# Gate and up columns of two feed-forward blocks: a new order of high-part and low-part matmuls

## What is computed

```python
def swiglu(h, w_gate, w_up, w_down):
    return (jax.nn.silu(h @ w_gate) * (h @ w_up)) @ w_down
...
    h = h + swiglu(rmsnorm(h, norm_ffn[i]), w_gate[i], w_up[i], w_down[i])
...
    h = rmsnorm_2(x, norm_ffn[i])
    up = dwconv3(h @ ffn_w_up[i], ffn_conv_w[i], ffn_conv_b[i])
    gate, val = jnp.split(up, 2, axis=-1)
    x = x + (jax.nn.silu(gate) * val) @ ffn_w_down[i]
```

## Time and profile before

| what | value |
|---|---|
| runs shown | 2710.66, 2700.53, 2703.84 us |
| median | 2703.84 us |
| profiled execution, its own time | 2710.54 us |
| its span | 2708.7 us |
| mean granted TensorE clock | 0.992 of full |
| TensorE busy | 2639.3 us (97%) |
| VectorE busy | 1924.6 us (71%) |
| ScalarE busy | 1495.4 us (55%) |

### The profile page before, as it was taken

One profiled execution on the slowest core, in us unless ns is written; L12 is line 12 of the kernel. 1 busy time (PEld: TensorE's weight loads), 2 busy tenths in 40 slices (PEclk: granted clock), 3 DMA queues, 4 the chain that ended last, 5 costly groups with the idle time before them and its releaser, 6 DMA issues.

```text
span 2708.7 us, 38546 instructions
## 1 busy us (share of the span) xinstructions
PE 2639.3 (97%) x14978; PEld 2276.8 (84%) x14978; DVE 1924.6 (71%) x2916; ACT 1495.4 (55%) x2307; POOL 393.6 (15%) x391
## 2 busy tenths in 40 slices
PE   7999999999998999999999999999999999999997
PEld 7888888888887888888888888888888888888886
DVE  8677786777787665656565679687877767676775
ACT  6555566768555444444444456535555555555554
POOL 3011100413411001010101033011101010101012
PEclk9999999999998999999999999999999999999999
DMA  7556666656554555666666656536566666666653
GB/s 247 163 184 183 184 196 193 188 184 188 172 177 133 168 162 172 188 192 187 188 191 189 188 162 211 167 117 187 179 194 190 190 188 189 190 189 189 189 179 121
DMA packets 135838, 490.76 MB, mean 181 GB/s; under 512 B 15207, under 2 KB 15528, under 8 KB 135656
## 3 DMA queue, kind: packets, MB, share of 16 engines
q1 hardware_dynamic: 135656, 488.31, 59.1%
HBM read 486.12 MB, written 2.13 MB: 180 GB/s over the span
## 4 chain that ended last, share of the span: by engine, by line
PE 87%; DVE 8%; ACT 2%; issue 2%; DMA 0%; DVEq 0%; ACTq 0%; SPq 0%
PE ps L708 56%; PE ps L710 28%; DVE wl L1195 3%; ACT wh L913 1%; DVE hT L1195 1%; DVE X L1201 1%; PE ps L849 0%; PE ps L882 0%; DVE R L1195 0%; DVE Gf L1195 0%; DVE T L1195 0%; DVE A L1201 0%; DVE A L1195 0%; DVE T L1201 0%; PE ps L795 0%
## 5 line engine op out<-in xcount | busy, mean ns | idle before, releaser
L1195 DVE TENSOR_TENSOR wl<-raw,wh 128x1024 fp32r<-128x1024 f32 x902 | 1140.8, 1269 | 710.3 <-ACT wh L913 709.6
L708 PE MATMUL ps<-X,wh 128*128 128x512 f32 x4848 | 1538.4, 399 | 5.5 <-DVE hT L1195 3.5
L913 ACT ACTIVATE wh<-raw 128x1024 fp32r<-128x1024 f32 x902 | 952.3, 1059 | 951.2 <-PE ps L710 931.0
L710 PEld LDWEIGHTS ps<-X,wl 128*128 128x128 f32 x4848 | 912.7, 188 | 215.1
L710 PE MATMUL ps<-X,wl 128*128 128x256 f32 x4848 | 955.7, 278 | 0.0
L708 PE MATMUL ps<-XG,wh 128*128 128x512 f32 x2304 | 734.1, 400 | 31.1 <-DVE hT L1195 17.0
L708 PEld LDWEIGHTS ps<-X,wh 128*128 128x128 f32 x4848 | 742.6, 189 | 20.1 <-issue 8.7
L710 PEld LDWEIGHTS ps<-XG,wl 128*128 128x128 f32 x2304 | 435.8, 189 | 103.4
L710 PE MATMUL ps<-XG,wl 128*128 128x256 f32 x2304 | 455.5, 279 | 0.0
L1650 POOL TENSOR_TENSOR hT<-hT,T 128x256 f32<-128x256 f32 x224 | 190.2, 870 | 1459.0 <-DVE hT L1195 1459.0
L708 PEld LDWEIGHTS ps<-XG,wh 128*128 128x128 f32 x2304 | 353.9, 190 | 39.1 <-DVE hT L1195 20.4
(11 more groups left out here) (168 smaller groups left out, 1105.2 us busy)
## 6 DMA issues: line engine op xcount, KB each, us to landing
raw<-in_w_gate SPq DMA_DIRECT2D x176, 512.0 KB, 3.7
raw<-in_w_down SPq DMA_DIRECT2D x176, 512.0 KB, 3.7
raw<-in_w_sc SPq DMA_DIRECT2D x96, 512.0 KB, 4.1
raw<-in_w_up SPq DMA_DIRECT2D x88, 512.0 KB, 3.6
raw<-in_w_val SPq DMA_DIRECT2D x88, 512.0 KB, 3.7
raw<-in_w_zx SPq DMA_DIRECT2D x80, 512.0 KB, 3.9
raw<-in_w_in SPq DMA_DIRECT2D x68, 512.0 KB, 3.7
raw<-in_w_osc SPq DMA_DIRECT2D x32, 512.0 KB, 3.7
```

The source lines that it names most:

```text
L708: e.matmul(bank(c, i)[:, :], wh[:, b0 + 128 * i:b0 + 128 * i + 128], x, start=st and kk == 0, stop=False)
L710: t = e.matmul(bank(c, i)[:, 0:256], wl[:, b0 + 128 * i:b0 + 128 * i + 128], x[:, 0:256], start=False, stop=sp and kk == c.kn - 1)
L913: return e.activation(out, in_, ACT.Copy, scale=scale)
L1195: return e.tensor_tensor(out, a, b, op)
```

## The change

Gate and up columns no longer issue their 16 matmuls in the loop that the other columns use. The unit first waits for all four activation tiles, and then takes its matmuls from a list of triples (kk, bank, low) that `orders` gives. The sums are the same sets of products; only their order in each bank differs. The first matmul into a bank is still H with kk = 0. The unit's last matmul still increments `mm`, and the stop flag is set at the last matmul of each bank.

```diff
+def orders(which, first):
+    start, rest = which % 5, which // 5
+
+    def alternate(ks):
+        if rest == 0:
+            return [(k, i, m) for k in ks for i in range(2) for m in range(2)]
+        return [(k, i ^ m, m) for i in range(2) for k in ks for m in range(2)]
+
+    if not first:
+        return alternate(range(4))
+    if start == 0:
+        return [(k, i, m) for m in range(2) for k in (0, 1) for i in range(2)] + alternate((2, 3))
...
+    if start == 2:
+        return [(0, 0, 0), (0, 1, 0), (1, 0, 0), (0, 0, 1), (0, 1, 1), (1, 0, 1), (1, 1, 0), (1, 1, 1)] + alternate((2, 3))
+    if start == 3:
+        return [(k, i, m) for m in range(2) for k in (0, 1, 2) for i in range(2)] + alternate((3,))
...
+ORDER_OF = [5, 0, 6, 1, 7, 2, 8, 3, 9, 4, 0, 9, 1, 8, 2, 7, 3, 6, 4, 5, 8, 1, 4, 7, 0, 3, 6, 9, 2, 5, 5, 3, 1, 9, 7, 6, 0, 2, 4, 8, 3, 2, 0, 5]
...
                 w.wait_ge(s, n)
+                if c.kind in ("gate", "up"):
+                    continue
...
+            if c.kind in ("gate", "up"):
+                order = orders(ORDER_OF[c.i], st)
+                ends = {i: n for n, (kk, i, low) in enumerate(order)}
+                for n, (kk, i, low) in enumerate(order):
+                    X, kx = xtile(c, g * c.kn + kk)[:2]
+                    b0 = (u % NW) * UN + kk * 256 + 128 * i
+                    if low:
+                        t = e.matmul(bank(c, i)[:, 0:256], wl[:, b0:b0 + 128], X[:, kx * 512:kx * 512 + 256], start=False,
+                                     stop=sp and n == ends[i])
+                    else:
+                        t = e.matmul(bank(c, i)[:, :], wh[:, b0:b0 + 128], X[:, kx * 512:kx * 512 + 512], start=st and kk == 0,
+                                     stop=sp and n == ends[i])
```

More of the change, by code:

```diff
@@ L383, in schedule @@
     return at
+def orders(which, first):
[8 more added lines that the diff above has]
+        return [(k, i, m) for m in range(2) for k in (0, 1) for i in range(2)] + alternate((2, 3))
+    if start == 1:
+        return [(k, i, m) for m in range(2) for k in (0, 1) for i in range(2)] + [(2, 0, 0), (2, 1, 0), (2, 0, 1), (3, 0, 0), (
+            2, 1, 1), (3, 1, 0), (3, 0, 1), (3, 1, 1)]
+    if start == 2:
+        return [(0, 0, 0), (0, 1, 0), (1, 0, 0), (0, 0, 1), (0, 1, 1), (1, 0, 1), (1, 1, 0), (1, 1, 1)] + alternate((2, 3))
+    if start == 3:
+        return [(k, i, m) for m in range(2) for k in (0, 1, 2) for i in range(2)] + alternate((3,))
+    return [(k, i, m) for m in range(2) for k in (0, 1) for i in range(2)] + [(2, i, m) for m in range(2) for i in range(2)] + alternate((3,))
+ORDER_OF = [5, 0, 6, 1, 7, 2, 8, 3, 9, 4, 0, 9, 1, 8, 2, 7, 3, 6, 4, 5, 8, 1, 4, 7, 0, 3, 6, 9, 2, 5, 5, 3, 1, 9, 7, 6, 0, 2, 4, 8, 3, 2, 0, 5]
 PLAN = schedule()
```

## The result

The changed kernel takes 2712.26 us (median of 19 runs, 2705.62 to 2716.89), beside 2707.18 us for the kernel before on the same chips (19 runs, 2700.53 to 2710.86). The ratio is 1.0020, with a 95% interval of 1.0012 to 1.0028. So it is slower by about 5 us, less than the 0.5% that counted as a difference, and about half of the 10.9 us that the sum gave.

A forecast was written before the change was run, and what follows sets the result against it. The prediction took TensorE to bound the gate and up stretches. Alternation added 10.9 us (10.6 in later units, 0.4 in first units), waits and bank nothing: 2703.84 + 10.9 = 2714.7 us, range 2697 to 2730 us.

The forecast's parts named there:

- The bound: Gate and up stretches: TensorE bounds them, busy 997.05 of 997.17 us; every nanosecond of pitch goes straight into the time.
- The time: Whole kernel: 2714.7 us, ratio 1.004; 2711 to 2718 given 50%, "same" (within 0.5%) given 0.64.
- The cost of alternation: Gate and up units: an alternating H and L pair costs 353.3 ns against 348.3, 40 ns a whole unit.
- The prediction's own sign of being wrong: Changed gate and up columns: the forecast is wrong if a pair over two banks has any pitch but 353 ns.
- The price by steps: Gate and up units: one more HL and LH replacing HH and LL costs 10.0 ns; 1094 more HL steps, +10.9 us.
- Bounds: Limits of the alternation term: -80 us from streaming alone, -5 us at the `v` stretch's price, +33 us from above.
- The bank: Gate and up pairs: one bank or two was given no price, but kept as a rival.
- Rival 1: Gate and up: only a pair on one bank is dear, kinds 5 to 9 pay nothing; +5.7, 2709.5 us; 14%.
- Rival 2: Gate and up columns: order has no effect, the 5 ns are peculiar to `dt`; 2703.8 us; chance 10%.
- Rival 3: Gate and up: L between two H hides its load better if the bank changes; 2699 or 2691 us; chance 10%.
- Rival 4: Gate and up: changing tile, weights and bank each step makes pairs 0.36 us; up to +33 us, 2737; chance 16%.
- Waits that move ahead: First gate column of each layer: activation tiles waited for up to 2.1 us earlier; price nothing.

## Why the prediction came out as it did

*The bound* was read rightly: TensorE's pitch in the gate and up stretches goes into the time one for one, with nothing to absorb it and nothing behind it. Stretches grew by 5.2 us, the runs by 5.1.

*The time* fell into the range of 2697 to 2730 us and into "same", but the difference to the kernel before is +5.1 us and not +10.9; the range was wide enough for either. That 2712.26 us lies in the narrower forecast of 2711 to 2718 is luck: the sum started from 2703.84 us, and the median of the kernel before over 19 runs is 2707.18.

*The cost of alternation* is the step that failed, as a term: "a pair costs 5.0 ns more", from the `dt` column's 353.3 against 348.3 ns, taken for all alternating pairs "because the work is the same". It measured +5.0 ns in the long columns (47 in the second to tenth stretches) and -1.7 ns in the short ones (31). The `dt` row was a fair sample of one rhythm of two, and no row of before showed the other. Fifteen steady pairs looked like fifteen observations; they were one, since a stream in a fixed cycle repeats itself. The rows as printed could not warn of it: pairs of 0.35, 0.36 and 0.35 us are also what a fixed 353.3 ns gives when start times are rounded to 0.01 us. The whole ns of the same trace could, since the pitches of H in `dt` go 232, 241, 235 and begin again. The prediction's own sign of being wrong, a pair over two banks at anything but 353 ns, did come: kind 9 runs at 346.7.

*The price by steps* (one more HL and LH costs 10.0 ns) went with it. It gave the first units +0.4 us; they cost +0.8 in the second to tenth stretches alone. Kind 4's first unit, with as many HL steps as HHLL has, is 7 ns shorter, and that of kind 3, with fewer, is 7 ns longer.

*Bounds.* The `v` stretch's lower bound of 346.6 ns a pair is what the short rhythm has (346.7), but its parts are not: the bound has 226.6 for H and 120 for L, the short rhythm 231.5 and 115, so the sum agrees by chance. Some two in five columns met the lower bound; the sum had put them at 353.3 like the others. All units of the kernel at that pitch would be 892 x -13.3 ns = -12 us, and no repeating order here came to under it.

*The bank* was rightly given no price: the run with one bank a pair changed no unit behind the first stretch but two of gate 22. Rival 1 came nearest in time (2709.5 on a median of 2703.8), and by the wrong mechanism. *Rival 2*, that the order has no effect, doesn't hold: the same 16 matmuls took 2773, 2787, 2793 or, on average, 2827 ns by their order and entry. The 325 ns a pair worked out from the formula for an isolated matmul in the Trainium skill ("TensorE: Matmul & The Clock Gate", section "Back-to-back issue gap") is below every repeating row here, whose shortest pair is 346.7 ns. *Rival 3* was right that something faster exists, for kinds 4 and 9, but by phase and not by bank. *Rival 4* didn't come: 0.36 us pairs exist only as one of three in the long rhythm.

*Waits that move ahead* cost nothing that can be seen: the only wait in the gate and up matmuls is 1.3 us ahead of the first gate column, where the kernel before waited 2.8 us.

## What to carry to other kernels

A steady stretch in a trace is one sample of the pattern it runs in, however long it is; before its price is used elsewhere, ask whether the pattern there is entered in the same way, and look for a cycle in the single pitches. Where an engine is bound by back-to-back instructions of two lengths, their order and the way into a repeating row can be worth 1.5% of the stretch (88.82 against 90.20 us), with no instruction more or less; a short lead-in that ends in the good phase is the whole edit. Here versions with such a lead-in beat both kernels (0.9980 to 0.9990 of the kernel before), but it must be tried, since a lead-in works only if it reaches that phase from every entry.

## What the runs showed of the hardware

- The pitch of fp32r matmuls with a weight load each, at the full clock, is not a constant of the instruction: in repeating rows an H (512 columns) took 227 to 241 ns and an L (256 columns) 112 to 120, by what had gone before. At half clock an H took 427 and an L 213 or 214, with no such spread, in HHLL at the start of the program.
- The cycles found are all multiples of 6.67 ns: 120 (a run of L), 226.7 (a run of H), 693.3 (short), 1060 (long), 1393.3 (two rounds HHLL). 6.67 ns is 16 cycles of 2.4 GHz, but this is read off the numbers only. What in the engine keeps such a step, and why there are two rhythms, was not tested.
- Two states can both be stable for the same instruction stream: HLHL ran at 346.7 or 353.3 ns a pair for three units on end, and changed only at a different order, a small matmul or a gap.
- The spread between executions of one kernel, 11 us here, goes with TensorE's granted clock: 0.991 in the two longest of the 19 (2716.89 and 2716.24 us), 0.996 in the two shortest (2705.62 and 2705.76).
